# Sparse attention: the selection mask is added to the bias by GpSimd, not to the logits by TensorE

## What is computed

```
score  = indexer(h)                          # which keys each query keeps
sel    = top_k(score, 256)                   # 256 keys per query
logits = q @ k_sel.T * HEAD_DIM ** -0.5
logits = logits + t5_table[bucket(sel - t)]  # relative bias, per head
p      = softmax(where(valid, logits, -inf))
o      = p @ v_sel
```

## Time and profile before

| what | value |
|---|---|
| median of 3 runs | 3085.7 us |
| the profiled execution: its own time | 3087.72 us |
| its span, first to last instruction | 3085.9 us |
| granted TensorE clock, mean | 0.960 of full speed |
| this attention, first to last unit | about 338 to 705 us from the start |
| its pairs: last row maximum of pair 0, 2, 4, 5 | 391.9, 479.7, 571.8, 620.5 us |

### The profile page before, as it was taken

The page is one execution under the profiler, slowest core; times in us unless marked ns, Lnnn a source line. Parts: engine busy times, 40 slices in busy tenths (PEclk is TensorE's granted clock), DMA queues, the critical chain, the costliest instruction groups (busy, mean ns, idle before and its releaser), DMA issues. The chain is left out here.

```text
span 3085.9 us, 38811 instructions
## 1 busy us (share of the span) xinstructions
PE 2813.5 (91%) x14642; PEld 2393.6 (78%) x14674; DVE 1706.4 (55%) x2824; ACT 1037.4 (34%) x1906; POOL 790.6 (26%) x417
## 2 busy tenths in 40 slices
PE   5879498999999999999888888888888999999999
PEld 4679387888788888888777877777776888888887
DVE  4699766661544445444556565556566544445444
ACT  4557455551322222222333333333334222222221
POOL 2031433302332232322331111121102322232322
PEclk9989699999999999999999999999989999999999
DMA  4010000011111111111110010000001111111111
GB/s 158 1 62 21 21 8 8 5 59 35 69 55 43 46 54 41 54 48 48 38 42 9 25 33 33 33 1 33 13 8 55 55 48 48 41 54 41 54 48 62
DMA packets 36310, 124.09 MB, mean 40 GB/s; under 512 B 3968, under 2 KB 12336, under 8 KB 34384
## 3 DMA queue, kind: packets, MB, share of 16 engines
q1 hardware_dynamic: 36176, 122.29, 11.4%
HBM read 118.03 MB, written 9.49 MB: 41 GB/s over the span
## 5 line engine op out<-in xcount | busy, mean ns | idle before, releaser
L330 PE MATMUL banks<-XH,WH 128*128 128x512 f32 x1408 | 436.9, 392 | 6.0 <-POOL WL L291 4.9
L330 PE MATMUL banks<-XL,WH 128*128 128x512 f32 x1408 | 434.9, 390 | 0.0
L330 PE MATMUL banks<-XH,WL 128*128 128x512 f32 x1408 | 434.9, 390 | 0.0
L291 POOL TENSOR_TENSOR WL<-WR,WH 128x1024 fp32r<-128x1024 f32 x132 | 331.1, 2516 | 368.8 <-ACT WH L245 368.8
L386 DVE TENSOR_TENSOR U<-banks,RB 128x1024 f32<-128x1024 f32 x88 | 107.7, 1224 | 407.6 <-PE banks L330 398.3
L260 ACT ACTIVATE Y<-U,CONVB,CONVW 128x1024 f32<-128x1024 f32 x88 | 109.5, 1244 | 633.0 <-DVE U L386 633.0
L330 PEld LDWEIGHTS banks<-XH,WH 128*128 128x128 f32 x1408 | 265.2, 189 | 62.9 <-POOL WL L291 5.0
L330 PEld LDWEIGHTS banks<-XL,WH 128*128 128x128 f32 x1408 | 265.4, 189 | 55.4
L330 PEld LDWEIGHTS banks<-XH,WL 128*128 128x128 f32 x1408 | 265.1, 188 | 55.3
L376 DVE TENSOR_TENSOR XT<-XT,banks 128x1024 f32<-128x1024 f32 x176 | 214.4, 1218 | 165.0 <-PE banks L346 165.0
L299 POOL TENSOR_TENSOR AL<-Y,AH 128x1024 fp32r<-128x1024 f32 x44 | 105.9, 2407 | 611.3 <-ACT AH L268 611.3
(11 more groups left out here) (216 smaller groups left out, 5628.7 us busy)
## 6 DMA issues: line engine op xcount, KB each, us to landing
WR<-in_ffn SPq DMA_DIRECT2D x132, 512.0 KB, 3.2
QWR<-in_qkv SPq DMA_DIRECT2D x12, 1536.0 KB, 7.5
XT<-in_xT SPq DMA_DIRECT2D x16, 512.0 KB, 6.8
OWR<-in_w_o SPq DMA_DIRECT2D x16, 512.0 KB, 3.7
outT<-XT SPq DMA_DIRECT2D x8, 512.0 KB, 2.6
near<-strip SPq DMA_DIRECT2D x1, 3072.0 KB, 26.0
BB<-near SPq DMA_DIRECT2D x8, 384.0 KB, 5.1
near<-strip SPq DMA_DIRECT2D x1, 2048.0 KB, 16.1
```

Of the source, the lines that this page charges most:

```text
L291: pool.tensor_tensor(WL[:, ch % RING, :], WR[:, ch % RING, :], WH[:, ch % RING, :].bitcast(F32), ALU.subtract).then_inc(w_lo, 1)
L330: mm = pe.matmul(u[:, h * HALF:(h + 1) * HALF], w[:, ch % RING, db * P:(db + 1) * P], x[:, db, h * HALF:(h + 1) * HALF], start=(db == 0 an ...
```

## The change

ScalarE first multiplies the mask by -1e30 in place, tile by tile (6 instructions). For each unit of tiles 2 to 7, GpSimd's new `join(g)` writes `BM`, one of two buffers: the mask alone, converted to f32, for the far keys (1 copy), and bias plus mask for the 256 near keys (1 addition). `row_max(g)` reads `BM` instead of `BB`, and waits for it. `logits` has only its two matmuls. `join` waits for the scaled mask, for the bias, and, from the third on, until `row_max` of the joined unit two before has read its buffer. `BB` keeps only 256 columns, so the memset is gone. 96 units are joined (12 in each pair).

```diff
-        BB = m.take("BB0", [P, 2, 2, S], F32)
+        BB = m.take("BB0", [P, 2, 2, W], F32)
+        BM = m.take("BM0", [P, 2, S], F32)
...
         @block.scalar
...
+            for i in range(FIRST_TOP, TT):
+                cols = MASK[:, SC_OFF[i]:SC_OFF[i] + SEEN[i]]
+                act.activation(cols, cols, ACT.Copy, scale=NEG).then_inc(scaled_mask, 1)
             queries_high(0, 0)
...
         @block.gpsimd
...
+            def join(g):
+
+                p, k, s, i, h = place(g)
+                if i < FIRST_TOP:
+                    return
+                n = (i + 1) * P
+                v = joined_before(g)
+                pool.wait_ge(b_masked, p + 1)
+                pool.wait_ge(scaled_mask, i - FIRST_TOP + 1)
+                if v >= 2:
+                    pool.wait_ge(max_done, joined_unit(v - 2) + 1)
+                mask = MASK[:, SC_OFF[i]:SC_OFF[i] + n]
+                pool.tensor_copy(BM[:, v % 2, 0:n - W], mask[:, 0:n - W])
+                pool.tensor_tensor(BM[:, v % 2, n - W:n], BB[:, p % 2, h, :], mask[:, n - W:n],
+                                   ALU.add).then_inc(b_joined, 1)
+
+            joined = [0]
+
+            def joins(upto):
+
+                for g in range(joined[0], upto):
+                    join(g)
+                joined[0] = max(joined[0], upto)
+
             raw_square(0)
             raw_square(1)
             for t in range(TT):
                 root(t)
                 scaled(t)
-                if t == 0:
-                    pool.memset(BB[:, :, :, 0:S - W], 0.0).then_inc(b_blank, 1)
                 if t + 2 < TT:
                     raw_square(t + 2)
+                joins(min(2 * t + 2, UNITS - 1))
             for k in range(1, GROUPS):
+                base = (2 * k - 2) * UNITS
                 for i in range(TT + 1):
                     if i < TT:
                         raw_square(k * TT + i)
                     if i >= 1:
                         root(k * TT + i - 1)
+                    if k == 1 and i % 2 == 1:
+                        joins(UNITS - 1 + i)
+                    if k > 1 and i < TT:
+                        joins(base + 2 * i + 5)
                 if k == 2:
                     output_weights(0)
                     output_weights(1)
+                base += UNITS
                 for i in range(TT):
                     scaled(k * TT + i)
+                    joins(base + 2 * i + 5)
+            joins(ALL)
...
         @block.tensor
...
-                    mm = pe.matmul(out, q, KL[:, k % 2, a:b], start=False, stop=i < FIRST_TOP)
-                    if i >= FIRST_TOP:
-                        mm = pe.matmul(out, c.IDN[:], MASK[:, SC_OFF[i] + a:SC_OFF[i] + b], start=False, stop=True)
+                    mm = pe.matmul(out, q, KL[:, k % 2, a:b], start=False, stop=True)
...
         @block.vector
...
+                bias = BB[:, p % 2, h, W - min(n, W):W]
+                if i >= FIRST_TOP:
+                    dve.wait_ge(b_joined, joined_before(g) + 1)
+                    bias = BM[:, joined_before(g) % 2, 0:n]
```

More of the change, by code:

```diff
@@ L1092, in dsa_phase @@
         b_landed = [sem("b_even"), sem("b_odd")]
-        b_blank, b_masked = sem("b_blank"), sem("b_masked")
+        b_masked, b_joined, scaled_mask = sem("b_masked"), sem("b_joined"), sem("scaled_mask")
         o_landed = [sem("o_even"), sem("o_odd")]
@@ L1140, in seconds_before, with joined_before, joined_unit @@
             return sum(place(v)[3] >= 4 for v in range(g))
+        joined_units = [g for g in range(ALL) if place(g)[3] >= FIRST_TOP]
+        def joined_before(g):
+            return sum(v < g for v in joined_units)
+        def joined_unit(v):
+            return joined_units[v]
         @block.sync
@@ L1147, in _ @@
             for p in range(2):
-                sp.dma_start(BB[:, p, :, S - W:S], near[p]).then_inc(b_landed[p], 16)
+                sp.dma_start(BB[:, p, :, :], near[p]).then_inc(b_landed[p], 16)
             for p in range(PAIRS_ - 2):
                 sp.wait_ge(max_done, UNITS * (p + 1))
-                sp.dma_start(BB[:, p % 2, :, S - W:S], near[p + 2]).then_inc(b_landed[p % 2], 16)
+                sp.dma_start(BB[:, p % 2, :, :], near[p + 2]).then_inc(b_landed[p % 2], 16)
             sp.wait_ge(pv_ready, 6 * UNITS)
@@ L1417, in mask @@
                 dve.wait_ge(b_landed[p % 2], 16 * (p // 2 + 1))
-                dve.memset(BB[0:HD, p % 2, :, S - HD:S], NEG).then_inc(b_masked, 1)
+                dve.memset(BB[0:HD, p % 2, :, W - HD:W], NEG).then_inc(b_masked, 1)
             def row_max(g):
@@ L1427, in row_max @@
                 dve.wait_ge(s_ready, g + 1)
-                dve.tensor_tensor_reduce(out=PR[:, g % AHEAD, 0:n], in0=LG[g % 2][:, 0:n],
-                                         in1=BB[:, p % 2, h, S - n:S], op0=ALU.add, op1=ALU.min, scale=-1.0,
-                                         scalar=PLUS, accum_out=NM[:, g % 8:g % 8 + 1]).then_inc(max_done, 1)
+                bias = BB[:, p % 2, h, W - min(n, W):W]
+                if i >= FIRST_TOP:
+                    dve.wait_ge(b_joined, joined_before(g) + 1)
+                    bias = BM[:, joined_before(g) % 2, 0:n]
+                dve.tensor_tensor_reduce(out=PR[:, g % AHEAD, 0:n], in0=LG[g % 2][:, 0:n], in1=bias, op0=ALU.add,
+                                         op1=ALU.min, scale=-1.0, scalar=PLUS,
+                                         accum_out=NM[:, g % 8:g % 8 + 1]).then_inc(max_done, 1)
             def output(o):
@@ L1447, in _ @@
             variance(2)
-            dve.wait_ge(b_blank, 1)
             mask(0)
```

## The result

The changed kernel takes 3129.8 us (median of 4 runs, 3128.4 to 3130.1) beside 3084.9 us for the kernel before (4 runs, 3083.2 to 3089.0): ratio 1.0143, 95% interval 1.0125 to 1.0160, 45 us slower. The forecast was 3118, with a range of 3097 to 3134. The profiled execution took 3130.1 us; its span is 42.5 us longer than that of before.

The account below looks back on a forecast made before the run. It took TensorE as the bound, with GpSimd free. Terms -15 (mask passes), +24 (pair 0), +1.7 (pair 0 to 1), +22 (pairs 2 and 4) gave +32.7 us: 3120.4 profiled, forecast 3118, range 3097 to 3134.

Parts of the forecast that it names:

- Pair 0: a chain through GpSimd: In pair 0, row maximum, join, root, scaled and round follow one another without overlap: +24 us (+14 at the high clock).
- First link: Pair 0, start of the chain: `queries` of tile 4 starts at 365.1 instead of 361.90, +3.2 us.
- Periods: Pair 0, three intervals between query rounds at 1.2 GHz: 10.0, 11.5, 13.0 us, against 5.0, 5.3, 5.3.
- The rest of the pair, with the step to pair 1: Pair 0 after the periods: +3 running slowly, -1.5 without mask passes; then +1.7 us as root waits behind two joins.
- the first rival: Pairs 0, 2 and 4: the chains hold but the clock stays high; +16.8 us, 3102; chance 0.22.
- A join: GpSimd's copy plus addition per unit: 0.84 us in tile 2 to 1.55 in tile 7, 14 us a pair.
- Pairs 2 and 4: a chain through VectorE: Row maximum waits for a join behind root, with `output` queued behind: six steps 36.4 us against 28.5; +11 a pair, +22.
- What goes: TensorE's mask passes: 3.0 us a pair saved, counted for pairs 1, 3, 5, 6 and 7 only, -15 us.
- The scalings on ScalarE: Start of the phase: six mask scalings, some 5.3 us on an idle ScalarE; at most a microsecond, once.
- Downstream nothing moves but the start: After the first attention: later work only starts at another time, with no further change.
- GpSimd's steps are dearer: Rival: joins 30% dearer, only 2.0 us a pair saved; +44 us, 3130; chance 0.12.

Follow-up runs that it names:

- the run with 128 pads: Changed kernel with 128 one-column matmuls that nobody reads put into TensorE's stream ahead of the second attention's loop; 3130.5 us, ratio 1.0142.
- all-three kernel: Changed kernel with pair 0's joins one tile later, pairs 2 and 4's joins ahead of the root, 160 small matmuls in the selection phase; 3069.1 us, ratio 0.9954.

## Why the forecast held, and what it missed

- **"Pair 0: a chain through GpSimd"**: right in kind and size. First link +3.2 forecast, +3.4 measured (364.58 - 342.14 against 361.90 - 342.87). Periods 10.0, 11.5 and 13.0 forecast, 10.9, 10.9 and 11.6 measured: 34.5 and 33.4 us in sum. The first was longer than I had and the last shorter: the tile's serial work, from its round to the row maximum, was 6.3, 6.2 and 6.6 us where I had 5.6, 6.9 and 8.2. The low clock did not hold "through these periods" but rose, to 0.70 on the mean after 372 us. The rest of the pair, with the step to pair 1, cost +5.6, not +3.2. The run with later joins shows that the order was the cause. (The 9.4 us for a period at the high clock is 0.6 below the sum of the terms given for it, 10.0; only the first rival uses it.)
- **"A join"**: forecast 0.84 to 1.55 us. Measured (groups of POOL by form, 336 to 790 us):

```profile
L1280 POOL TENSOR_TENSOR BM<-BB,MASK 128x256 f32<-128x256 f32 x96 | 64.5, 672 | 0.0
...
L1279 POOL CAST BM<-MASK 128x768 f32<-128x768 bf16 x16 | 13.2, 824 | 17.4 <-DVE NM L1473 17.4
...
L1279 POOL CAST BM<-MASK 128x128 f32<-128x128 bf16 x16 | 4.6, 289 | 5.7 <-DVE NM L1473 5.7
```

  0.96 us in tile 2, 1.50 in tile 7, so 14.8 us a pair against 14 forecast. The addition took 0.67 us, where I had 0.60.
- **"Pairs 2 and 4: a chain through VectorE"**: the six steps took 5.1, 5.4, 6.2, 6.5, 6.8 and 6.4 us, 36.3 in sum; 5.0, 5.2, 5.6, 6.8, 7.1 and 6.7 forecast, 36.4. Mis-sized was what the low clock adds: I took +3 a pair, measured +8.7 and +9.2 in all against +7.9 without it. The granted clock was 0.87 in pair 2.
- **"What goes"**: 3.0 us a pair. Pairs 1, 3, 5, 6 and 7 gave 13.2 of the 15 us, and the kernel with the passes taken out alone gave 23.8 for eight, just 3.0 each.
- The scalings on ScalarE, costed at nothing: six in 4.19 us from 337.70, done before its first copy at 343.30.
- The sum for the attention is nearer than its terms: pair 0 with its step to pair 1 came 1.2 us above the forecast, pairs 2 and 4 together 4.1 below, and the saving was 1.8 short. That they cancel to 1.0 is luck.
- **"Downstream nothing moves but the start"** is the step that failed. The profiles are 42.5 us apart where the sum had 32.7: +11.0 in the second attention, -1.0 in the first. I read the second attention as unchanged, since its code is, and did not ask what 160 fewer instructions do to where its loop lies in the stream. That 3130 still lies in the range is luck too, since its upper part was set aside for dearer joins. The rival "GpSimd's steps are dearer" had given 3130, but for a reason that the rows above deny.

What stalls at the loop's return is shown only from outside. One of the profile's queues of instruction transfers, q8, which by its times I take for TensorE's, moves a packet of 16 KB at a time: for 1500 to 2400 us of the changed kernel

```profile
q8 instruction: 39, 0.64, 0.3%
```

In slices of one microsecond, one such packet runs at 1822 and the next at 1827 to 1828, while TensorE idles from 1824.27 to 1829.62; in the kernel before they run at 1791 and at 1795, and TensorE is already at work from 1793.66. There it doesn't need the second packet yet; in the changed kernel it starts only behind it. So it is at both returns in all 14 profiles: the two packets always run, in the eight kernels with stalls TensorE starts 2.2 to 2.6 us after the start of the second, and in the six without before it. Behind the stall the granted clock is lower too: 0.64 from 1829 to 1836 us, where the kernel before has 1.00 from 1793 to 1800. The Trainium skill, Runtime: NRT & Kernel Launch, section Instruction fetch mechanics, says that instructions are fetched in blocks of 16 KiB, 256 instructions, and that a taken branch whose target isn't held waits for the fetch. The trace agrees (0.64 MB in 39 packets is 16.4 KB each), and so does the run with 128 pads, which was chosen by that figure: same place in a block, same stalls. That every return waits for a first block and only a loop head near the end of one waits for a second is my reading; it fits all places tried (stalls at two lengths 256 apart and none at three others), but no run varied the place finely. In each stall the second packet falls into the transfers for the next group, which SP issues at the same moment; whether they hold it up wasn't tried.

## What to carry over

Before putting work on an idle engine, look at what stands behind it in that engine's list: the joins cost 27 us in pair 0 and 9 in each of pairs 2 and 4 because they stood ahead of a step that the bound engine waits for; with three calls of `joins` moved, these pairs take 60.1, 48.8 and 44.2 us, just under what they took before the change. An engine at 29% can be the critical one in a chain. And an edit that changes how many instructions an engine runs ahead of a hardware loop can move the time of that loop, though its code is unchanged: look for idle stretches put down to "issue" at its returns before crediting or blaming the edit.

## What the hardware showed besides

In the kernels with the joins ahead of the root, VectorE's smallest instruction, a `tensor_scalar` on 5 columns, is held up. Before, all 32 took 170 to 173 ns. The tile's group in the kernel before, then in the all-three kernel:

```profile
L1393 DVE TENSOR_SCALAR QVAR<-SSQ x32: 170/172/173, 340.1 to 579.7; 128x5 f32<-128x5 f32 x32
```

```profile
L1434 DVE TENSOR_SCALAR QVAR<-SSQ x32: 171/172/1956, 339.7 to 572.8; 128x5 f32<-128x5 f32 x32
```

The longest, with the GpSimd instructions of that time (timelines of DVE and POOL, all-three kernel):

```profile
467.32 1.96 DVE L1434 TENSOR_SCALAR QVAR<-SSQ 128x5 f32<-128x5 f32 x1
469.19 0.68 DVE L1507 COPY PT<-banks 128x512 f32<-128x512 f32 x1
```

```profile
467.19 0.67 POOL L1280 TENSOR_TENSOR BM<-BB,MASK 128x256 f32<-128x256 f32 x1
467.81 0.82 POOL L1279 CAST BM<-MASK 128x768 f32<-128x768 bf16 x1
468.59 0.67 POOL L1280 TENSOR_TENSOR BM<-BB,MASK 128x256 f32<-128x256 f32 x1
469.36 1.18 POOL L1248 TENSOR_TENSOR RS<-QVAR,NHALF 128x5 f32<-128x5 f32 x1
```

It ends with GpSimd's last back-to-back instruction (468.59 + 0.67), having been held through three of them, and the 32 cost 6.7 us more than before (12.2 against 5.5). The row maxima, with one operand in PSUM and one in SBUF, keep their durations (1223 ns for 1024 columns, 1224 in the earlier trace rows). The Trainium skill, SBUF — State Buffer, section Who interferes with whom, says that VectorE and GpSimd share one pair of SBUF ports, that a `tensor_scalar` can run in a mode that takes this pair, where one engine waits until the other's instruction is over, and that an instruction with at most one SBUF input, outside such a mode, doesn't contend. The trace agrees on both, with the 1956 ns above and the unchanged 1223 ns. That the wait lasts over several GpSimd instructions in a row is seen here. I had not costed it. It may be part of why the all-three kernel keeps its distance to the kernel with no passes and no joins; how large a part was not measured.
